# Expert weight slots loaded by partition halves instead of row halves

## The reference

```
gl = h @ w_grp + b_grp;  el = h @ w_exp + b_exp        # 4 groups, 8 experts each
gate, expert_id = top group, then its top 2 experts     # 2 of 32 experts a token
expert_block(xb, e) = (silu(xb @ w_gate[e]) * (xb @ w_up[e])) @ w_down[e]
out[token] += gate * expert_block(h[token], e)
```

## Time and profile before

| | us |
|---|---|
| median of 3 runs | 1940.54 (1937.41 to 1941.0) |
| profiled execution | 1939.81 |
| its span, first to last instruction | 1938.1 |
| PE busy in the span | 1874.7 (97%) |
| mean granted clock of TensorE | 0.988 |

### The profile page before, as it was taken

The page is one execution under the profiler, slowest core; times in us unless marked ns, Lnnn a source line. Parts: engine busy times, 40 slices in busy tenths (PEclk is TensorE's granted clock), DMA queues, the critical chain, the costliest instruction groups (busy, mean ns, idle before and its releaser), DMA issues.

```text
span 1938.1 us, 18367 instructions
## 1 busy us (share of the span) xinstructions
PE 1874.7 (97%) x7560; PEld 923.1 (48%) x7560; DVE 584.0 (30%) x1097; ACT 374.2 (19%) x627; POOL 157.3 (8%) x144
## 2 busy tenths in 40 slices
PE   6999999997999999999999999999979999999997
PEld 5445644544444454444443444454444544444443
DVE  3899211223122222222212322213222222222223
ACT  2333211212111111111113232122111111111113
POOL 0566110010000000000020000100100000000001
PEclk9999999998999999999999999999989999999998
DMA  9214422202999999999761211302059999999992
GB/s 360 71 47 169 159 87 87 87 4 87 403 403 409 412 404 414 405 413 408 319 220 44 87 44 44 130 0 90 29 227 403 406 413 405 412 407 415 405 412 101
DMA packets 89771, 476.96 MB, mean 246 GB/s; under 512 B 7614, under 2 KB 8044, under 8 KB 40140
## 3 DMA queue, kind: packets, MB, share of 16 engines
q1 hardware_dynamic: 88636, 470.90, 60.6%
q0 software_dynamic: 496, 2.53, 0.5%
q10 hardware_dynamic: 544, 2.22, 0.3%
HBM read 471.43 MB, written 4.19 MB: 245 GB/s over the span
## 4 chain that ended last, share of the span: by engine, by line
PE 89%; DVE 8%; ACT 1%; issue 1%; DMA 0%; DVEq 0%; SPq 0%; ACTq 0%
PE PS L601 23%; PE PS L430 16%; PE PS L386 13%; PE PS L616 12%; PE PS L639 7%; PE PS L654 7%; DVE PS L1718 5%; PE PS L892 3%; PE PS L525 2%; PE PS L437 1%; PE PS L549 1%; PE PS L646 1%; PE PS L628 1%; PE PS L663 1%; DVE PS L1716 1%
## 5 line engine op out<-in xcount | busy, mean ns | idle before, releaser
L430 PE MATMUL PS<-hT,ring 128*128 128x512 f32 x640 | 277.7, 593 | 4.2 <-issue 3.4
L616 PE MATMUL PS<-ring,hT 128*64 128x512 f32 x1024 | 226.8, 595 | 2.7 <-ACT hT L1217 2.7
L601 PE MATMUL PS<-ring,hT 128*64 128x512 f32 x1024 | 226.3, 595 | 1.3 <-DVE small L1598 1.3
L601 PE MATMUL PS<-ring,xg 128*64 128x512 f32 x1024 | 226.8, 595 | 0.0
L1607 DVE TENSOR_TENSOR xT<-PS,xT 128x512 f32<-128x512 f32 x256 | 159.3, 682 | 212.7 <-PE PS L639 212.6
L430 PEld LDWEIGHTS PS<-hT,ring 128*128 128x128 f32 x640 | 120.8, 190 | 152.2 <-issue 151.1
L601 PEld LDWEIGHTS PS<-ring,hT 128*64 128x64 f32 x1024 | 73.8, 137 | 133.1 <-issue 131.4
L601 PEld LDWEIGHTS PS<-ring,xg 128*64 128x64 f32 x1024 | 72.2, 137 | 132.6 <-issue 132.4
L616 PEld LDWEIGHTS PS<-ring,hT 128*64 128x64 f32 x1024 | 70.7, 137 | 135.1 <-issue 127.9
L1633 DVE TENSOR_TENSOR ylo<-PS,yhi 128x1024 fp32r<-128x1024 f32 x32 | 39.2, 1224 | 301.6 <-ACT yhi L1222 301.6
L639 PE MATMUL PS<-onehotT,yhi 128*128 128x512 f32 x256 | 116.0, 453 | 3.6 <-DVE ylo L1633 3.6
(11 more groups left out here) (259 smaller groups left out, 1767.3 us busy)
## 6 DMA issues: line engine op xcount, KB each, us to landing
ring<-in_moe_w_gate SPq DMA_DIRECT2D x128, 1024.0 KB, 11.4
ring<-in_moe_w_up SPq DMA_DIRECT2D x128, 1024.0 KB, 12.2
ring<-in_moe_w_down SPq DMA_DIRECT2D x128, 1024.0 KB, 9.2
ring<-in_xa_w_kv SPq DMA_DIRECT2D x16, 1024.0 KB, 7.5
ring<-in_gla_w_in SPq DMA_DIRECT2D x12, 1024.0 KB, 13.0
ring<-in_conv_w_in SPq DMA_DIRECT2D x8, 1024.0 KB, 14.4
ring<-in_xa_w_q SPq DMA_DIRECT2D x8, 1024.0 KB, 6.7
ring<-in_xa_w_o SPq DMA_DIRECT2D x8, 1024.0 KB, 6.9
```

The lines of the kernel that those rows point to most:

```text
L430: mm = pe.matmul(bank(b), w[:, k * 512 + m * P:k * 512 + (m + 1) * P], src[:, k, :], start=(k == 0), stop=(k == C - 1))
L601: mm = pe.matmul(PS[e * SL:(e + 1) * SL, kind * BANK:(kind + 1) * BANK], x[:, k, (2 * (p % 2) + e) * SL:(2 * (p % 2) + e + 1) * SL], ring[ ...
L616: mm = pe.matmul(PS[e * SL:(e + 1) * SL, (2 + half) * BANK:(3 + half) * BANK], hidT[:, k, e * SL:(e + 1) * SL], ring[:, pair_slot(l, 4 + e ...
```

## The change

The two halves of a slot are now partitions 0 to 63 and partitions 64 to 127, each with the whole 16 KB of a partition; a DMA is 1 MiB as before. For the whole-slot order, TensorE waits for all four DMAs of a kind at k = 0 of a pass, and counts gate_full and up_full once at the end of a pass; SP waits once per kind, before h = 0, for the whole pass of the pair before. ACT's, DVE's and the closing waits count 1 per pair instead of 2. The other stages' loads stay as they were.

```diff
--- before.py
+++ after.py
@@ -594,23 +594,24 @@
                 def up(p, kind, key):
                     x = xg[(p // 2) % 2]
                     for k in range(C):
-                        if k % 4 == 0:
+                        if k == 0:
                             for e in range(2):
-                                loaded(p, 2 * kind + e, k // 4)
+                                for h in range(2):
+                                    loaded(p, 2 * kind + e, h)
                         for e in range(2):
                             mm = pe.matmul(PS[e * SL:(e + 1) * SL, kind * BANK:(kind + 1) * BANK],
                                            x[:, k, (2 * (p % 2) + e) * SL:(2 * (p % 2) + e + 1) * SL],
                                            ring[:, pair_slot(l, 2 * kind + e), k * 512:(k + 1) * 512],
                                            start=(k == 0), stop=(k == C - 1))
-                        if k % 4 == 3:
-                            mm.then_inc(g[key], 1)
+                    mm.then_inc(g[key], 1)
 
                 def down(p):
                     pe.wait_ge(g["hidT_ready"], NP * r + p + 1)
                     for k in range(FC):
-                        if k % 2 == 0:
+                        if k == 0:
                             for e in range(2):
-                                loaded(p, 4 + e, k // 2)
+                                for h in range(2):
+                                    loaded(p, 4 + e, h)
                         for half in range(2):
                             for e in range(2):
                                 mm = pe.matmul(PS[e * SL:(e + 1) * SL, (2 + half) * BANK:(3 + half) * BANK],
@@ -950,16 +951,15 @@
                             sp.wait_ge(*first_wait[2 * kind + e])
                     for h in range(2):
                         if p or first_wait is None:
-                            if kind < 2:
-                                sp.wait_ge(g[key], 2 * NP * r + (2 * p - 1 + h))
-                            elif h == 0:
+                            if h == 0:
                                 sp.wait_ge(g[key], NP * r + p)
                         for e in range(2):
                             slot = pair_slot(l, 2 * kind + e)
                             w = a[("moe_w_gate", "moe_w_up", "moe_w_down")[kind]][l, 2 * p + e]
                             nk = C if kind < 2 else FC
-                            w = w.rearrange("(p k) n -> p k n", p=P)[:, h * nk // 2:(h + 1) * nk // 2, :]
-                            sp.dma_start(dst_half(slot, h).rearrange("p (k n) -> p k n", k=nk // 2),
+                            rows = slice(h * SL, (h + 1) * SL)
+                            w = w.rearrange("(p k) n -> p k n", p=P)[rows]
+                            sp.dma_start(ring[rows, slot, :].rearrange("p (k n) -> p k n", k=nk),
                                          w).then_inc(ld[slot][h], 16)
 
             vector_rows(sp, list(VROWS)[:NFIRST], s_vfirst)
@@ -971,8 +971,7 @@
                         sp.wait_ge(*full(release[n - RING]))
                     elif n >= RING:
                         j = n - RING - moe_base[l - 1] - RING * (NP - 1)
-                        sp.wait_ge(*((seg[l - 1]["gate_full"], 2 * NP), (seg[l - 1]["up_full"], 2 * NP),
-                                     (seg[l - 1]["y_full"], NP))[j // 2])
+                        sp.wait_ge(seg[l - 1][("gate_full", "up_full", "y_full")[j // 2]], NP)
                     if l == 1 and t == tiles[1][2]:
                         sp.wait_ge(moe_done, 1)
                     for h in range(2):
@@ -992,7 +991,7 @@
                     with sp.Fori(1, ROUNDS) as r:
                         for p in range(NP):
                             pair_loads(l, p, ov_ld[l], None, r)
-                    for key, n in (("gate_full", 2 * NP), ("up_full", 2 * NP), ("y_full", NP)):
+                    for key, n in (("gate_full", NP), ("up_full", NP), ("y_full", NP)):
                         sp.wait_ge(seg[l][key], n * ROUNDS)
             o_dram = out.rearrange("b (t p) d -> (b t) p d", p=P)
             for t in range(TT):
@@ -1210,7 +1209,7 @@
                 for p in range(NP):
                     q, s = p // 2, p % 2
                     more = q + 1 < NQ
-                    act.wait_ge(g["gate_full"], 2 * NP * r + (2 * p + 2))
+                    act.wait_ge(g["gate_full"], NP * r + p + 1)
                     act.wait_ge(g["gates_ready"], NP * r + p + 1)
                     act.activation(sil, bank(0), ACT.Silu, scale=rslot).then_inc(g["silu_done"], 1)
                     act.wait_ge(g["ht_full"], NP * r + p + 1)
@@ -1624,7 +1623,7 @@
                     if p:
                         accumulate(p, range(0, 4))
                     dve.wait_ge(g["silu_done"], NP * r + p + 1)
-                    dve.wait_ge(g["up_full"], 2 * NP * r + (2 * p + 2))
+                    dve.wait_ge(g["up_full"], NP * r + p + 1)
                     dve.scalar_tensor_tensor(hidden, sil, gcol, bank(1), ALU.mult,
                                              ALU.mult).then_inc(g["hidden_ready"], 1)
                     if p:
```

## The result

| | before | after |
|---|---|---|
| median, us | 1940.77 (4 runs) | 2799.48 (4 runs, 2791.9 to 2804.58) |
| span of the profiled execution, us | 1938.1 | 2790.2 |
| mean granted clock of TensorE | 0.988 | 0.856 |

The ratio is 1.4416, 95% interval 1.4385 to 1.4447. The forecast was 2807 us; the profiled execution took 2791.9.

What follows compares the result with a forecast made beforehand. TensorE was taken to bound the kernel, by one microsecond in thirty over the loads; at half rate the loads would take over. Own time 1939.8 + 857 for loads + 10 for the clock = 2807 us, range 2000 to 2975.

Steps and rivals of the forecast that it cites:

- The slack of one microsecond in thirty: Experts' part: a pair's loads take 29.8 us of TensorE's 30.83 us; loads slower than 408 GB/s would take over.
- The later release: SP's gate and up loads go out 3.4 us later; hidden by TensorE's passes, cost 0, bounds 0 and 3.4 us per layer's start-up.
- the waits and counts: TensorE's mid-pass test of h = 1 moves to the pass's start: saves 0, bounded by zero and 10 us.
- the longer runs: Runs of 16 KB instead of 8 KB: worth 0 to 2% of a load, buying no time as TensorE bounds the part.
- The destination: Experts' loads write 64 partitions, not 128: 211 GB/s taken, 422 if engines set the pace; 59.6 us a pair; half rate 0.70.
- half the partitions take half: Experts' loads: if the way into the partitions sets the rate, 64 of them take 211 GB/s (216 with longer runs).
- The sum: Whole kernel: own time 1939.8 us, plus 857 for both layers' loads, plus 10 for the clock, gives 2807 us.
- the loads' term: Pairs 1 to 15 load for 894.6 us a layer; last down passes come 428.5 and 428.6 us later, together 857 us.
- The clock: After each layer's last down load TensorE runs 10 us at half speed, costing 5 us, twice: 10 us.
- Rival 2, engines out of step: Experts' loads: some engines write the upper half while others write the lower; 316 GB/s, 39.8 us a pair, 2212 us; chance 0.12.
- Signs: Trace after, experts' parts: DMA share near 1.00 at 211 GB/s, TensorE half idle, period 59.6 us, landings 20 to 40 us.

Runs made afterwards that it cites:

- the four kernels that loaded whole slots at a full rate: Changed kernel with: 128-partition 8 KB-run loads, 1940.12 us; one 2 MiB load a slot, 1939.62; even/odd partitions, 1939.25; contiguous source into even/odd partitions, 1940.59.
- release-only: Changed kernel with its waits and counts kept, but each load again writing all 128 partitions in runs of 8 KB: 1940.12 us, ratio 0.9997.
- whole-slot: Changed kernel with each slot as one 2 MiB load over all 128 partitions in runs of 16 KB: 1939.62 us, ratio 0.9995.
- parity: Changed kernel with the two halves of a slot as even and odd partitions instead of lower and upper: 1939.25 us, ratio 0.9994.
- the two mixed kernels: Changed kernel with one side by parity: DRAM source only, partitions still by halves, 2790.72 us; destination only, source still contiguous, 1940.59 us.
- quarters: Changed kernel with each slot in four loads of 32 neighbouring partitions, 0.5 MiB each: 2814.19 us, ratio 1.4493.
- the middle alone: Changed kernel loading only partitions 32 to 95 of every slot, the other half of each weight left out: 1938.49 us, one run.
- two-queue kernel: Changed kernel with lower halves loaded by SP's queue and upper halves by ACT's queue for pairs 1 to 15: 2498.18 us, ratio 1.2876.

## Why the prediction was right

*The slack of one microsecond in thirty.* Right: the experts' part passed from TensorE to the loads, and each of the four kernels that loaded whole slots at a full rate came back to 1940 us.

*The later release, the waits and counts, the longer runs.* Priced at 0 each. The release-only and the whole-slot kernels show it, within 0.2% each. What makes the later release free, by my working, is the backlog that keeps the queue filled meanwhile; no run takes the backlog away to test that.

*The destination.* I took half of 422, 211 GB/s, against a bound of 422 that the trace did not exclude. It was 213. The choice was one between two ends, given 0.70; the rows of before could not make it, since all large loads there went to 128 partitions. The reason that I gave from rows, a rate that stays at 418 to 431, would fit engines that run at a pace of their own as well, so as far as the rows go the right end was in part luck. And my rule for that end, "half the partitions take half", is too simple: it holds for these halves and not for the even partitions or the middle. Now it rests on runs: parity against halves (2095 against 1168 us of engine time for the same packets), and the two mixed kernels that put it on the write side. The Trainium skill's port map (SBUF — State Buffer, Door 1: The DMA port swizzle) had said it: by its formula partitions 0 to 63 reach 8 of 16 ports, 0 to 31 the same 8, and 32 to 95 all. The quarters (212 GB/s), the middle alone (426) and parity (full rate) agree with it. Of the two figures that the prediction quotes from that page for half the ports, the asymptote of 218 GB/s is near the 213 measured; the 196 of a load of 1 MiB is 8% under it.

*The sum, 2807 against 2791.9 for the profiled execution.* The lines that close it (PE's timeline of the changed kernel, last down pass of each layer, and TensorE's next matmuls on ring weights after layer 0's):

```profile
1379.52 10.08 PE L617 MATMUL PS<-ring,hT 128*64 128x512 f32 x32 [7.24 <-DMA ring<-in_moe_w_down]
...
1400.75 13.97 PE L430 MATMUL PS<-hT,ring 128*128 128x512 f32 x32 [3.10 <-ACT hT L1115]
...
2755.03 8.41 PE L617 MATMUL PS<-ring,hT 128*64 128x512 f32 x32 [6.72 <-DMA ring<-in_moe_w_down]
```

Layer 0's last down pass was forecast for 1384.6 and began at 1379.52, 5.1 us sooner: from 490.0 on, 15 periods of 59.3 us on average instead of 59.6. Layer 1 began its stream at the release of 1860.61 (the issue row of its first gate) + 2.6, and its last down pass at 2755.03: 891.8 us, 2.8 less than the forecast 894.6. That is the rate, 213 instead of 211. From 5.1 + 2.8 = 7.9 the loads' term becomes 849 instead of 857.

*The clock.* The mechanism was there and its size was off. The last down passes took 10.08 and 8.41 us instead of 7.09, so 3.0 and 1.3 us. What reached the end was less. The last down pass of layer 0 began 423.4 us later than before, and layer 1's first gate pass ended 424.6 later (1860.61 against 1432.60 + 3.4 = 1436.0), +1.2. The last pass of layer 1 began 850.4 later and the span ended 852.1 later, +1.7. Together 2.9 us against 10. I had taken the stretch after a stall ahead of the experts, 10 us at 0.50, for every stall; but after the stalls of 5 to 10 us here the passes took 8.4 to 10.1 us, of which only a part was at the lower level (1.2 GHz). Windows over the last down pass of layer 0 and of layer 1 show the part:

```profile
1379.50:1385.50 6.00, 5.98 (x14) 1.91 (x16) 0.00 (x0) 0.00 (x0) 0.00 (x0) 0.50 1.05 388
1385.50:1389.60 4.10, 4.10 (x21) 1.35 (x17) 0.00 (x0) 0.00 (x0) 0.00 (x0) 0.99 0.61 228
...
2755.00:2757.60 2.60, 2.57 (x6) 0.85 (x8) 0.00 (x0) 0.00 (x0) 0.00 (x0) 0.50 0.00 0
2757.60:2763.40 5.80, 5.80 (x29) 1.94 (x25) 0.00 (x0) 0.00 (x0) 0.00 (x0) 0.99 0.00 0
```

So 6.0 and 2.6 us at half speed, not 10. Why 1.8 of layer 0's 3.0 us had gone by layer 1's first gate pass was not traced. 7.9 + 7.1 = 15.0 us is the whole difference to 2807, in one execution; the four executions after lie 12.7 us apart, so the last microseconds of this account are a reading of this trace and no more.

*Rival 2, engines out of step.* Not what happened to the change, which ran at 213 GB/s. The two-queue kernel shows that something like it exists, at 252 GB/s rather than the 316 that I had assumed.

*Signs.* Landing times were forecast at 20 to 40 us; their median was 40.1, the longest 50.3, as the queue held up to two kinds and the rest of a third. TensorE was to idle about half of the time and was idle for 39% of a pair (busy 36.17 of 59.05 us), since the passes' own lengths changed, with the clock. The other stages kept theirs within a microsecond or two, as forecast.

## What to carry to other kernels

A load into a part of the partitions is to be judged by which ones it reaches: here neither their number nor the length of the runs decided, but halves 0 to 63 and 64 to 127 ran at half rate, even and odd partitions at full rate. Where a slot has to be filled in two loads, the halves by parity did it at no cost (1939.25 us). Where a period of 30.83 us hides 29.8 us of loads, read the engine time of the queue (share times span) beside the rate, since a share near 1.00 looks the same at 408 and at 213 GB/s. Release order and run length, which the edit was about, were both worth nothing within 0.2% in this kernel, where TensorE hides the loads; the side effect was worth 44%.

## What the runs showed of the hardware that was not expected

- A mix of a full-pace load (partitions 32 to 95) with one-sided ones began at 278 GB/s, as their paces alone make it, and was at 197 some 200 us later, with the engines as busy (0.99). Over most of a layer it ran at 225 and 209 GB/s in one order of the loads and at 235 and 231 in the other (layer 0, layer 1), so the order matters by 4 to 11%. The cause is open.
- Two queues, each filling one half, reached 252 GB/s over layer 0's experts and not at once (231 in the first slice, 285 at most), 18% more than one queue, though the profile counts the same 16 engines for both.
- The granted clock over layer 0's experts was 0.79, with TensorE stalled three times a pair, mostly for 5 to 10 us.
- The profile's DMA share is 1.01 at 213 GB/s and 1.01 at 424: so it doesn't leave out an engine that its destination holds up, which the prediction had named as unknown.
